# A column operand for the partial sums, maxima negated as they are taken, and a wait of GpSimd on the scaled queries

## The chip, the cores and the metric

The kernel runs on one core of a Trainium2 chip. The metric is the device time of one execution in microseconds (us), as the median of several runs. Engines go by the profile's names: PE is TensorE (PEld its weight loads), DVE is VectorE, ACT is ScalarE, POOL is GpSimd, SP is SyncE.

## What is computed

One inference step of a small hybrid backbone: two layers on 128 context tokens and 512 latent tokens (five tiles of 128 tokens, tile 0 the context), model width 1024. Each layer has a global attention (branch a), a windowed attention with a sink logit per head (branch b) and a gated MLP (branch c), merged by sigmoid gates. The part that matters here is the softmax of the attentions, cut to its core:

```python
qa = apply_rope(rms_norm(br['qa'], lw['q_norm']), cos, sin)
s = jnp.einsum('bqkgd,blkd->bkgql', qblk, k).astype(jnp.float32)
if sink is not None:
    s = jnp.concatenate([s, col], axis=-1)
p = jax.nn.softmax(s, axis=-1)
return jnp.einsum('bkgql,blkd->bqkgd', p.astype(v.dtype), v)
```

## The kernel before

**Products in two halves.** Every large product is made in a 32-bit matmul format whose operands are split in a high and a low half, three matmuls for one (lines 872 to 874, and 924). A unit of weights (128 x 1024) is loaded by SP into one of three raw buffers, rounded by ACT to `w_hi` (line 1130, `split_hi`), and POOL subtracts: `w_lo` = raw - `w_hi` (line 1749, event `split`). The halves lie in a ring of four slots, and PE waits on `w_ready` before it uses a unit.

**The order.** All engines walk one list of events, `ORDER`, and each does its part of an event and waits on semaphores for the rest; so the queue of every engine is fixed when the kernel is built. A wait holds back everything behind it on that engine. `with_splits` places the split events between the others, some events after the ring slot's last use.

**One attention group** (`attention`): ten groups per branch and layer, one for each of two key heads and five query tiles, with four query heads each. For a group of latent queries:
- event `S`: PE makes the scores of a unit in PSUM; units are the cached keys of all four heads (branch a only), then one for each head. DVE takes the maximum (line 1600) and makes its negative, combined with the maximum over the cached keys or the sink (line 1602, one column out, a column as operand). ACT waits for that column and takes the exponential (`ex`, line 1292), with the row sum as a side output; the part over cached keys or the sink has a sum of its own (lines 1284, 1287).
- event `iv`: DVE adds the two partial sums of a head (line 1610) and takes the reciprocal (line 1611); POOL multiplies the probabilities by it (line 1772, tile `p_f_a` or `p_f_b`).
- event `T`: PE waits until all heads of the group are scaled and transposes them (line 1075); ACT copies to `p_hi` (line 1303), DVE makes the rest `p_lo` (line 1616, event `pl`), which also frees the PSUM bank; there are two banks for `T`. `PV` (lines 1086, 1087) is two steps behind `T`. The product's sums go through lines 1310 and 1624 to `o_sum`.

Chunks of gate products (line 924) are mixed in as filler. The last two groups, of the context tile, have one unit `heads` with all four heads: DVE reads the maxima of four heads at once (line 1594), in branch b joins the sinks (line 1596), and negates (line 1597).

```python
after(did(dve.tensor_reduce(best, by_head(ps[:, s, :]), axis=AX.X, op=ALU.max)))
if br == "b":
    after(did(dve.tensor_tensor(best, best, sinks, ALU.max)))
did(dve.tensor_scalar(neg[:, c, :], best, -1.0, None, ALU.mult), neg_made)
```

**The queries.** In `queries_or_keys` DVE rotates the projected queries out of PSUM and writes `q_st`: in branch a it sums squares (line 1435), POOL makes the root (`root`, lines 1732 and 1733), and DVE multiplies (line 1449); in branch b it adds (line 1455). Either raises `staged`. PE then transposes `q_st` (line 1036, event `qt`), and ACT (line 1266) and DVE (line 1578) take the halves. There are ten such writes in a layer, five per branch.

Of the kernel before, what the change touches and what calls it, by code (L numbers as in the profile page):

```python
# [10 lines left out]
ALU = mybir.AluOpType  # L11
ACT = mybir.ActivationFunctionType
AX = mybir.AxisListType
# [10 lines left out]
GRP = 4  # L24
# [535 lines left out]
NO = numbers()  # L560
# [58 lines left out]
def build(nc, a, outs):  # L619
    with ExitStack() as ctx:  # L620
# [44 lines left out]
        neg = sb("neg", [P, 3, GRP])  # L665
        sums = sb("sums", [P, 3, 2, GRP])
# [67 lines left out]
        ps = ctx.enter_context(nc.psum_tensor("ps", [P, BANKS, 512], F32))  # L734
# [18 lines left out]
        sq_ready, v_hi_made, staged = sem("sq_ready"), sem("v_hi_made"), sem("staged")  # L753
        k_hi_made, q_hi_made = sem("k_hi_made"), sem("q_hi_made")
        neg_made, inv_made, over_sum = (sem(n) for n in ("neg_made", "inv_made", "over_sum"))
# [9 lines left out]
        class Tally:  # L765
# [5 lines left out]
            def did(self, instruction, semaphore=None):  # L771
                s = semaphore or self.step
                instruction.then_inc(s, 1)
                self.n[s.name] = self.n.get(s.name, 0) + 1
                return s, self.n[s.name]
# [40 lines left out]
        def by_head(tile):  # L816
            return tile.rearrange("p (h n) -> p h n", h=GRP)
# [10 lines left out]
        with nc.Block() as block:  # L828
# [532 lines left out]
            def _(dve):  # L1361
                tally = Tally(dve_step)
                did = tally.did
# [3 lines left out]
                def after(token):  # L1367
                    dve.wait_ge(*token)
# [93 lines left out]
                for e in ORDER:  # L1462
                    kind = e[0]
# [119 lines left out]
                    elif kind == "S":  # L1583
# [6 lines left out]
                        if unit == "cache":  # L1590
                            did(dve.tensor_reduce(others, by_head(ps[:, s, :]), axis=AX.X, op=ALU.max), neg_made)
                            dve.wait_ge(neg_made, NEG_NO[e])
                        elif unit == "heads":
                            after(did(dve.tensor_reduce(best, by_head(ps[:, s, :]), axis=AX.X, op=ALU.max)))
                            if br == "b":
                                after(did(dve.tensor_tensor(best, best, sinks, ALU.max)))
                            did(dve.tensor_scalar(neg[:, c, :], best, -1.0, None, ALU.mult), neg_made)
                        else:
                            h, n = unit, len(group_slots(br, g)) - (br == "a")
                            after(did(dve.tensor_reduce(best[:, h:h + 1], ps[:, s, 0:n * P], axis=AX.X, op=ALU.max)))  # L1600
                            other = others[:, h:h + 1] if br == "a" else sinks[:, h:h + 1]
                            did(dve.tensor_scalar(neg[:, c, h:h + 1], best[:, h:h + 1], other, -1.0, ALU.max, ALU.mult), neg_made)
                    elif kind == "iv":
# [2 lines left out]
                        heads = slice(0, GRP) if unit == "heads" else slice(unit, unit + 1)  # L1606
                        wait_drained(dve, ("S",) + e[1:])
                        total = sums[:, c, 0, heads]
                        if br == "b" or unit != "heads":
                            after(did(dve.tensor_tensor(total, total, sums[:, c, 1, heads], ALU.add)))  # L1610
                        did(dve.reciprocal(inv[:, c, heads], total), inv_made)  # L1611
                    elif kind == "pl":
# [108 lines left out]
            @block.gpsimd  # L1721
            def _(pool):
                tally = Tally(pool_step)
                did = tally.did
                asked = [0]

                def root(out, src, eps, first=0):
                    asked[0] += 1
                    pool.wait_ge(var_ready, asked[0])
                    n = out.shape[-1]  # L1730
                    mine = with_eps[:, first:first + n]
                    pool.wait_ge(*did(pool.tensor_scalar(mine, src, eps, None, ALU.add)))
                    did(pool.tensor_tensor(out, mine, minus_half[:, 0:n], ALU.pow), rstd_ready)

                def shift(t):
                    pool.wait_ge(rstd_ready, asked[0])
                    pool.wait_ge(*did(pool.tensor_tensor(nmr[:, t:t + 1], mv[:, t, 0:1], rstd[:, t:t + 1], ALU.mult)))
                    did(pool.tensor_scalar(nmr[:, t:t + 1], nmr[:, t:t + 1], -1.0, None, ALU.mult), nmr_ready)

                did(pool.memset(silu_c[:, :, :], 0.0), zeroed)  # L1740
                did(pool.memset(minus_half[:, :], -0.5), zeroed)
                pool.wait_ge(zeroed, 2)
                for e in ORDER:
                    kind = e[0]
                    if kind == "split":
                        n = e[1]
                        r, _ = raw_at(SPLIT_LOAD[n])
                        pool.wait_ge(hi_made, n + 1)
                        did(pool.tensor_tensor(w_lo[:, n % RING, :], raw_tile(r), w_hi[:, n % RING, :], ALU.subtract),  # L1749
                            w_ready)  # L1750
                    elif kind == "ln" and e[1]:
                        _, l, t = e
                        root(rstd[:, t:t + 1], mv[:, t, 1:2], EPS, t)
                        shift(t)
                    elif kind == "ln" and e[1] == 0:
                        for t in ARRIVAL:
                            root(rstd[:, t:t + 1], mv[:, t, 1:2], EPS, t)
                            if t in XN_ON_ACT:
                                shift(t)
                    elif kind in ("ln", "vn"):  # L1760
                        root(rstd[:, :], rstd[:, :], EPS)
                    elif kind == "in" and e[2] in ("q_a", "kv_a"):
                        heads = NKV if e[2] == "kv_a" else HEADS
                        c = NO[("sq", e)] % 2
                        root(rqk[:, c, 0:heads], ssq[:, c, 0:heads], HD * EPS)
                    elif kind == "iv":
                        _, l, br, g, i = e
                        c, unit = GROUP_NO[e[1:4]] % 3, score_units(br, g)[i]
                        heads = slice(0, GRP) if unit == "heads" else slice(unit, unit + 1)
                        part = p_part(br, g)[:, heads, :]  # L1770
                        pool.wait_ge(inv_made, NO[e] + 1)
                        did(pool.tensor_tensor(part, part, inv[:, c, heads].unsqueeze(2).to_broadcast(list(part.shape)), ALU.mult),  # L1772
                            over_sum)
                    elif kind == "og":
                        _, l, br, g = e
                        n = NO[e]
                        wait_drained(pool, ("O",) + e[1:])
                        wait_drained(pool, ("gT", l, br, 2 * GROUPS[g][0] + 1))
                        did(pool.tensor_tensor(og_sum(n), og_sum(n), og_part(g_t, g), ALU.mult), og_ready)
                    elif kind == "ol":  # L1780
                        _, l, br, g = e
                        n = NO[e]
                        pool.wait_ge(o_hi_made, O_MADE[e])
                        did(pool.tensor_tensor(og_part(o_lo, g), og_sum(n), og_part(o_hi, g), ALU.subtract), o_done)
                    elif kind == "y" and e[2] >= 1:
                        _, l, r, j = e
                        wait_drained(pool, e)
                        did(pool.tensor_tensor(merge[:, j, :], merge[:, j, :], gy[:, j % 2, :], ALU.add), merged)  # L1788
                    elif kind == "keep":
                        _, l, n = e  # L1790
                        r, _ = raw_at(KEEP_LOAD[e])
                        pool.wait_ge(keep_hi_made, KEPT[KEEP_LOAD[e]] + 1)
                        did(pool.tensor_tensor(kept_lo[n][:, :], raw_tile(r), kept_hi[n][:, :], ALU.subtract), kept)
                    elif kind == "out" and e[2] == 1 and e[1:] != (DEPTH - 1, 1, T - 1):
                        _, l, _, t = e
                        wait_drained(pool, e)
                        pool.wait_ge(x_alpha, T * l + t + 1)
                        did(pool.tensor_tensor(x[:, t, BW:D], x[:, t, BW:D], scaled[:, t % 2, :], ALU.add), x_summed)
                    elif kind == "st":
                        _, l, t = e  # L1800
                        root(rstd[:, t:t + 1], mv[:, t, 1:2], EPS, t)
                    elif kind == "hl":
                        _, l, t = e
                        pool.wait_ge(hh_ready, KT_D + t + 1)
                        did(pool.tensor_tensor(h_lo[:, :, t * P:(t + 1) * P], hf_of[:, :, :],
                                               h_hi[:, :, t * P:(t + 1) * P], ALU.subtract), h_ready)
# [110 lines left out]
```

## Time and profile before

| | |
|---|---|
| median of 3 runs | 1471.08 us (1470.16 to 1475.82) |
| the profiled execution | 1472.22 us, of which the span is 1470.1 us |
| PE busy | 1392.7 us, 95% of the span |
| POOL busy | 704.0 us, 48% |
| DVE busy | 726.2 us, 49% |
| ACT busy | 638.3 us, 43% |
| the chain that ended last | PE 79%, DVE 4%, POOL 3%, ACT 2%, issue 2% |
| costliest group off PE | line 1749, POOL, 148 splits, 358.1 us |
| granted TensorE clock, mean | 0.987 |

The busy share of an engine is an average over the span; the time of the kernel can only fall where PE stands idle, or runs at a low clock. So the profile is read for PE's idle stretches first: each has a place, a length and a releaser.

### The profile page before, as it was taken

To read this page: it belongs to the slowest core of one execution; us is meant where nothing else is said; L and a number is where in the kernel's file an instruction comes from. 1 tells how busy PE (TensorE), PEld (TensorE's weight loads), DVE (VectorE), ACT (ScalarE), POOL (GpSimd) and SP (SyncE) were. 2 spreads that over 40 slices of the span, in tenths; PEclk is the share of its full clock that TensorE was granted. 3 is DMA by queue.
4 is the path that set the end of the run, shared out by engine and by line. 5 is a ranking of instruction groups with operands and counts; after the bars stand their busy time and mean duration, and the time that the engine had idled before them with its cause. 6 is when DMAs were issued, how large, how long until landed. Compare 5 with 4: busy or idle time off the path is not lost.

```text
span 1470.1 us, 22567 instructions
## 1 busy us (share of the span) xinstructions
PE 1392.7 (95%) x8816; PEld 1276.4 (87%) x8816; DVE 726.2 (49%) x1412; ACT 638.3 (43%) x1298; POOL 704.0 (48%) x520
## 2 busy tenths in 40 slices
PE   5999999999999999999979999999999999999996
PEld 3898989889898898999868988897989989999985
DVE  4687774363663501413774767734546625031057
ACT  4345875335874211224143377752267733121230
POOL 2456665324565334344674556642246453444453
PEclk9999999999999999999989999999999999999999
DMA  8412001122013244343321210011111031225321
GB/s 332 146 47 82 20 30 44 62 72 72 30 44 107 92 147 165 108 186 122 111 98 35 85 58 30 24 63 63 58 59 44 30 129 44 86 72 187 115 87 72
DMA packets 36763, 126.96 MB, mean 86 GB/s; under 512 B 5041, under 2 KB 5681, under 8 KB 36657
## 3 DMA queue, kind: packets, MB, share of 16 engines
q1 hardware_dynamic: 29952, 108.54, 20.9%
q10 hardware_dynamic: 6704, 16.97, 3.2%
q8 instruction: 71, 1.16, 0.3%
q14 instruction: 36, 0.29, 0.1%
HBM read 119.73 MB, written 5.77 MB: 85 GB/s over the span
## 4 chain that ended last, share of the span: by engine, by line
PE 79%; DVE 4%; POOL 3%; ACT 2%; issue 2%; DVEq 0%; POOLq 0%; ACTq 0%
PE ps L924 45%; PE ps L872 6%; PE ps L874 6%; PE ps L873 6%; PE ps L1075 4%; PE ps L1059 3%; PE ps L1061 2%; PE ps L1086 2%; PE ps L1087 2%; POOL w_lo L1749 1%; PE ps L941 1%; ACT p_f_a L1292 1%; PE ps L1094 1%; POOL p_f_a L1772 1%; PE ps L1066 1%
## 5 line engine op out<-in xcount | busy, mean ns | idle before, releaser
L1749 POOL TENSOR_TENSOR w_lo<-raw,w_hi 128x1024 fp32r<-128x1024 f32 x148 | 358.1, 2426 | 361.4 <-ACT w_hi L1130 361.2
L924 PE MATMUL ps<-h_hi,w_hi 128*128 128x320 f32 x1280 | 298.1, 314 | 11.5 <-DVE g_c L1632 3.6
L924 PE MATMUL ps<-h_lo,w_hi 128*128 128x320 f32 x1280 | 293.0, 310 | 0.0
L924 PE MATMUL ps<-h_hi,w_lo 128*128 128x320 f32 x1280 | 292.9, 310 | 0.0
L924 PEld LDWEIGHTS ps<-h_hi,w_hi 128*128 128x128 f32 x1280 | 218.0, 189 | 31.5 <-issue 9.1
L924 PEld LDWEIGHTS ps<-h_hi,w_lo 128*128 128x128 f32 x1280 | 215.7, 189 | 1.7
L924 PEld LDWEIGHTS ps<-h_lo,w_hi 128*128 128x128 f32 x1280 | 215.3, 188 | 1.6
L1130 ACT ACTIVATE w_hi<-raw 128x1024 fp32r<-128x1024 f32 x148 | 153.5, 1054 | 103.8 <-DMA raw<-in_weights 50.5
L1647 DVE TENSOR_TENSOR gy<-ps,sg 128x640 f32<-128x640 f32 x32 | 26.4, 824 | 241.3 <-PE ps L924 241.3
L1600 DVE TENSOR_REDUCE top<-ps 128x1 f32<-128x512 f32 (+1 forms) x128 | 83.9, 655 | 111.3 <-PE ps L1066 78.1
L872 PE MATMUL ps<-w_hi,h_hi 128*128 128x512 f32 (+1 forms) x360 | 130.2, 362 | 4.1 <-POOL w_lo L1749 2.2
L874 PE MATMUL ps<-w_hi,h_lo 128*128 128x512 f32 (+1 forms) x360 | 128.6, 357 | 0.0
L873 PE MATMUL ps<-w_lo,h_hi 128*128 128x512 f32 (+1 forms) x360 | 128.5, 357 | 0.0
L1772 POOL TENSOR_TENSOR p_f_a<-p_f_a,inv 128x640 f32<-128x640 f32 (+1 forms) x68 | 84.3, 1241 | 80.4 <-DVE inv L1611 80.4
L1343 ACT ACTIVATE sg<-ps,pack 128x640 f32<-128x640 f32 x32 | 25.4, 795 | 210.6 <-PE ps L924 210.5
L1772 POOL TENSOR_TENSOR p_f_b<-p_f_b,inv 128x512 f32<-128x512 f32 (+1 forms) x68 | 62.9, 940 | 77.6 <-DVE inv L1611 77.6
L1303 ACT ACTIVATE p_hi<-ps 128x512 fp32r<-128x512 f32 x144 | 85.6, 594 | 31.8 <-PE ps L1075 28.4
L924 PE MATMUL ps<-o_hi,w_hi 128*128 128x320 f32 x384 | 91.4, 320 | 6.9 <-DVE rot_s L1392 6.0
L1788 POOL TENSOR_TENSOR merge<-merge,gy 128x640 f32<-128x640 f32 x32 | 51.2, 1600 | 85.8 <-DVE gy L1647 85.7
L924 PE MATMUL ps<-o_lo,w_hi 128*128 128x320 f32 x384 | 88.7, 312 | 0.0
L924 PE MATMUL ps<-o_hi,w_lo 128*128 128x320 f32 x384 | 88.5, 312 | 0.0
L1059 PE MATMUL ps<-k_hi,q_t 128*128 128x128 f32 (+2 forms) x224 | 81.6, 381 | 7.2 <-ACT p_f_b L1292 4.2
(178 smaller groups left out, 2674.0 us busy)
## 6 DMA issues: line engine op xcount, KB each, us to landing
raw<-in_weights SPq DMA_DIRECT2D x190, 512.0 KB, 3.3
raw_more<-in_weights SPq DMA_DIRECT2D x10, 512.0 KB, 10.6
x<-in_x_sample ACTq DMA_DIRECT2D x6, 512.0 KB, 8.6
x_mid<-x ACTq DMA_DIRECT2D x5, 512.0 KB, 2.6
x<-x_mid ACTq DMA_DIRECT2D x5, 512.0 KB, 6.4
y_sample<-x SPq DMA_DIRECT2D x3, 512.0 KB, 2.9
pack<-in_pack ACTq DMA_DIRECT2D x2, 528.0 KB, 4.6
x<-in_x_sample SPq DMA_DIRECT2D x2, 512.0 KB, 4.9
```

The source lines that it names most:

```text
L872: pe.matmul(out, st_hi, mv_hi, start=start, stop=False)
L873: pe.matmul(out, st_hi, mv_lo, start=False, stop=False)
L874: return pe.matmul(out, st_lo, mv_hi, start=False, stop=stop)
L924: last = pe.matmul(ps[:, s + half, 0:HALF], w[:, u % RING, cols], acts[:, k, half * HALF:(half + 1) * HALF], start=k == 0 and part == 0, s ...
L1059: pe.matmul(ps[:, s, col:col + width], q_t[:, head, t * P:(t + 1) * P], k_hi[:, kv, src], start=True, stop=False)
L1075: last = pe.transpose(ps[:, s, h * P:(h + 1) * P], p_part(br, g)[:, h, i * P:(i + 1) * P], ident)
L1130: did(act.activation(w_hi[:, n % RING, :], raw_tile(r), ACT.Copy), hi_made)
L1303: did(act.activation(p_hi[:, n % 3, :], ps[:, s, :], ACT.Copy), p_hi_made)
L1600: after(did(dve.tensor_reduce(best[:, h:h + 1], ps[:, s, 0:n * P], axis=AX.X, op=ALU.max)))
L1749: did(pool.tensor_tensor(w_lo[:, n % RING, :], raw_tile(r), w_hi[:, n % RING, :], ALU.subtract), w_ready)
L1772: did(pool.tensor_tensor(part, part, inv[:, c, heads].unsqueeze(2).to_broadcast(list(part.shape)), ALU.mult), over_sum)
L1788: did(pool.tensor_tensor(merge[:, j, :], merge[:, j, :], gy[:, j % 2, :], ALU.add), merged)
```

## The change

Three edits, all inside the walks of DVE and POOL:

- In branch a the maxima of the context tile are written negated by the reduction itself, and the second instruction goes. In branch b the reduction stays, and one instruction per head joins the sink (a column operand) and negates, four in place of two.
- The two partial sums of one head are added by `tensor_scalar` with the second sum as a column operand, in place of `tensor_tensor`.
- POOL waits, at each event of projected queries, until DVE has written `q_st`. Everything behind it in POOL's queue waits too, the next split above all.

```diff
@@ -1591,10 +1591,13 @@
                             did(dve.tensor_reduce(others, by_head(ps[:, s, :]), axis=AX.X, op=ALU.max), neg_made)
                             dve.wait_ge(neg_made, NEG_NO[e])
                         elif unit == "heads":
-                            after(did(dve.tensor_reduce(best, by_head(ps[:, s, :]), axis=AX.X, op=ALU.max)))
-                            if br == "b":
-                                after(did(dve.tensor_tensor(best, best, sinks, ALU.max)))
-                            did(dve.tensor_scalar(neg[:, c, :], best, -1.0, None, ALU.mult), neg_made)
+                            if br == "a":
+                                did(dve.tensor_reduce(neg[:, c, :], by_head(ps[:, s, :]), axis=AX.X, op=ALU.max, negate=True), neg_made)
+                            else:
+                                after(did(dve.tensor_reduce(best, by_head(ps[:, s, :]), axis=AX.X, op=ALU.max)))
+                                for h in range(GRP):
+                                    last = dve.tensor_scalar(neg[:, c, h:h + 1], best[:, h:h + 1], sinks[:, h:h + 1], -1.0, ALU.max, ALU.mult)
+                                did(last, neg_made)
                         else:
                             h, n = unit, len(group_slots(br, g)) - (br == "a")
                             after(did(dve.tensor_reduce(best[:, h:h + 1], ps[:, s, 0:n * P], axis=AX.X, op=ALU.max)))
@@ -1606,7 +1609,9 @@
                         heads = slice(0, GRP) if unit == "heads" else slice(unit, unit + 1)
                         wait_drained(dve, ("S",) + e[1:])
                         total = sums[:, c, 0, heads]
-                        if br == "b" or unit != "heads":
+                        if unit != "heads":
+                            after(did(dve.tensor_scalar(total, total, sums[:, c, 1, heads], None, ALU.add)))
+                        elif br == "b":
                             after(did(dve.tensor_tensor(total, total, sums[:, c, 1, heads], ALU.add)))
                         did(dve.reciprocal(inv[:, c, heads], total), inv_made)
                     elif kind == "pl":
@@ -1759,10 +1764,14 @@
                                 shift(t)
                     elif kind in ("ln", "vn"):
                         root(rstd[:, :], rstd[:, :], EPS)
+                    elif kind == "in" and e[2] == "q_b":
+                        pool.wait_ge(staged, NO[e] + 1)
                     elif kind == "in" and e[2] in ("q_a", "kv_a"):
                         heads = NKV if e[2] == "kv_a" else HEADS
                         c = NO[("sq", e)] % 2
                         root(rqk[:, c, 0:heads], ssq[:, c, 0:heads], HD * EPS)
+                        if e[2] == "q_a":
+                            pool.wait_ge(staged, NO[e] + 1)
                     elif kind == "iv":
                         _, l, br, g, i = e
                         c, unit = GROUP_NO[e[1:4]] % 3, score_units(br, g)[i]
```

DVE's queue in the attention of branch a, layer 0, where the third head's sum of a group is added and the next group's cached keys come in; before (`sums` are the row sums, `inv` their reciprocals, `drained` a PSUM bank given back):

```order
L1616 TENSOR_TENSOR p_lo_last<-ps,p_hi 128x512 [waits p_hi_made]
L1610 TENSOR_TENSOR sums<-sums 128x1 [waits drained1]
L1611 RECIPROCAL inv<-sums 128x1 [waits dve_step]
L1624 TENSOR_TENSOR o_sum<-ps,o_sum 64x256 [waits o_low_made,filled4]
L1624 TENSOR_TENSOR o_sum<-ps,o_sum 64x256 [waits o_low_made]
L1591 TENSOR_REDUCE top<-ps 128x4 [waits filled1]
L1616 TENSOR_TENSOR p_lo_a<-ps,p_hi 128x512 [waits p_hi_made,neg_made]
L1610 TENSOR_TENSOR sums<-sums 128x1 [waits drained0]
L1611 RECIPROCAL inv<-sums 128x1 [waits dve_step]
```

In the changed kernel the same rows stand there in the same order and with the same waits, but those of L1610 read `TENSOR_SCALAR sums<-sums 128x1` (L1613 there); nothing moved.

DVE's queue at the context tile of branch a, layer 0, before:

```order
L1611 RECIPROCAL inv<-sums 128x1 [waits dve_step]
L1594 TENSOR_REDUCE top<-ps 128x4 [waits filled0]
L1597 TENSOR_SCALAR neg<-top 128x4 [waits dve_step]
L1594 TENSOR_REDUCE top<-ps 128x4 [waits filled1]
L1597 TENSOR_SCALAR neg<-top 128x4 [waits dve_step]
L1616 TENSOR_TENSOR p_lo_a<-ps,p_hi 128x512 [waits p_hi_made]
L1616 TENSOR_TENSOR p_lo_last<-ps,p_hi 128x512 [waits p_hi_made]
```

and now:

```order
L1616 RECIPROCAL inv<-sums 128x1 [waits dve_step]
L1595 TENSOR_REDUCE neg<-ps 128x4 [waits filled0]
L1595 TENSOR_REDUCE neg<-ps 128x4 [waits filled1]
L1621 TENSOR_TENSOR p_lo_a<-ps,p_hi 128x512 [waits p_hi_made]
L1621 TENSOR_TENSOR p_lo_last<-ps,p_hi 128x512 [waits p_hi_made]
```

Two instructions are gone, and the first `p_lo` stands right behind the reductions.

POOL's queue at the queries of branch a, layer 0, now (before, the rows are the same without `staged`):

```order
L1737 TENSOR_SCALAR with_eps<-ssq 128x8 [waits var_ready,staged]
L1738 TENSOR_TENSOR rqk<-with_eps,minus_half 128x8 [waits pool_step]
L1754 TENSOR_TENSOR w_lo<-raw,w_hi 128x1024 [waits hi_made,staged]
L1737 TENSOR_SCALAR with_eps<-ssq 128x8 [waits var_ready]
L1738 TENSOR_TENSOR rqk<-with_eps,minus_half 128x8 [waits pool_step]
L1754 TENSOR_TENSOR w_lo<-raw,w_hi 128x1024 [waits hi_made,staged]
```

Of the 20 added waits, 16 fall on a split (3 and 5 in branch a of layers 0 and 1, 4 and 4 in branch b), two on a root, and two are followed at once by another wait. PE's, ACT's and SP's queues are the same in both kernels.

## Rows read from the trace of the kernel before

**Rows 1.** Whom PE waited for, whole run: us in total, times, longest us.
```profile
PE ps L1075 <- POOL p_f_a L1772: 5.4, 4, 2.4
...
PE ps L1036 <- DVE q_st L1449: 1.3, 1, 1.3
...
PE ps L1075 <- DVE p_lo_last L1616: 0.5, 2, 0.2
```

**Rows 2.** Timeline around 181 to 188 us, all engines: start, us, engine, line, operation [idle before].
```profile
181.20 2.38 POOL L1749 TENSOR_TENSOR w_lo<-raw,w_hi 128x1024 fp32r<-128x1024 f32 x1
...
181.35 2.25 DVE L1610 TENSOR_TENSOR sums<-sums 128x1 f32<-128x1 f32 x1
...
182.73 0.59 ACT L1303 ACTIVATE p_hi<-ps 128x512 fp32r<-128x512 f32 x1
...
184.94 0.46 PE L924 MATMUL ps<-h_hi,w_lo 128*128 128x320 f32 x2
...
185.34 0.69 DVE L1616 TENSOR_TENSOR p_lo_a<-ps,p_hi 128x512 fp32r<-128x512 f32 x1
...
186.37 1.25 POOL L1772 TENSOR_TENSOR p_f_a<-p_f_a,inv 128x640 f32<-128x640 f32 x1 [1.24 <-DVE inv L1611]
...
187.77 0.63 PE L1075 MATMUL ps<-ident_r,p_f_a 128*128 128x128 f32 x4 [2.37 <-POOL p_f_a L1772]
```

**Rows 3.** Lines 1610 and 1602, all instances: ns min/median/max, first and last start, forms.
```profile
L1610 DVE TENSOR_TENSOR sums<-sums x132: 130/150/2256, 132.1 to 1175.5; 128x1 f32<-128x1 f32 x128, 128x4 f32<-128x4 f32 x4
...
L1602 DVE TENSOR_SCALAR neg<-top x64: 212/214/215, 129.3 to 945.0; 128x1 f32<-128x1 f32 x64
L1602 DVE TENSOR_SCALAR neg<-top,pack x64: 212/214/217, 348.0 to 1162.9; 128x1 f32<-128x1 f32 x64
```

**Rows 4.** Timeline, 134 to 135.5 us, POOL and DVE.
```profile
134.13 1.25 POOL L1772 TENSOR_TENSOR p_f_a<-p_f_a,inv 128x640 f32<-128x640 f32 x1 [0.38 <-DVE inv L1611]
...
134.91 0.21 DVE L1602 TENSOR_SCALAR neg<-top 128x1 f32<-128x1 f32 x1
135.06 0.34 DVE L1610 TENSOR_TENSOR sums<-sums 128x1 f32<-128x1 f32 x1
```

**Rows 5.** Timeline, 221 to 230 us: the context tile of branch a, layer 0.
```profile
223.72 2.39 POOL L1749 TENSOR_TENSOR w_lo<-raw,w_hi 128x1024 fp32r<-128x1024 f32 x1
223.72 2.41 DVE L1597 TENSOR_SCALAR neg<-top 128x4 f32<-128x4 f32 x1
...
226.05 0.68 DVE L1616 TENSOR_TENSOR p_lo_a<-ps,p_hi 128x512 fp32r<-128x512 f32 x1
...
226.78 0.66 PE L1075 MATMUL ps<-ident_r,p_f_a 128*128 128x128 f32 x4 [1.50 <-DVE p_lo_a L1616]
```

**Rows 6.** Three stretches: us, busy us of PE, PEld, DVE, ACT, POOL; PEclk, DMA, GB/s.
```profile
187.77:226.78 39.01, 37.51 (x247) 34.68 (x247) 30.29 (x73) 30.53 (x87) 24.46 (x21) 1.00 0.04 15
913.65:954.26 40.61, 39.11 (x246) 35.99 (x247) 30.28 (x73) 30.65 (x87) 24.48 (x21) 0.96 0.04 14
849.30:856.10 6.80, 6.80 (x27) 6.55 (x27) 2.68 (x5) 2.77 (x4) 4.68 (x2) 0.51 0.30 91
```

**Rows 7.** Timeline, 843.5 to 852 us: the last queries of branch a, layer 1.
```profile
844.09 2.79 DVE L1449 TENSOR_TENSOR q_st<-rot_c,rqk 128x512 f32<-128x512 f32 x1 [1.46 <-POOL rqk L1733]
...
847.03 0.63 PE L1036 MATMUL ps<-ident_r,q_st 128*128 128x128 f32 x4 [1.27 <-DVE q_st L1449]
847.25 1.41 DVE L1578 SCALAR_TENSOR_TENSOR q_t<-ps,q_t 64x512 fp32r<-64x512 f32 x2 [0.37 <-ACT q_t L1266]
...
848.76 0.53 PE L924 MATMUL ps<-h_hi,w_hi 128*128 128x320 f32 x2 [1.11 <-issue]
```

**Rows 8.** Line 1449, all instances: ns min/median/max, first and last start, form.
```profile
L1449 DVE TENSOR_TENSOR q_st<-rot_c,rqk x10: 693/2809/2827, 72.5 to 844.1; 128x512 f32<-128x512 f32 x10
```

**Rows 9.** Timeline: a split of branch a's queries and PE's first use.
```profile
90.10 2.40 POOL L1749 TENSOR_TENSOR w_lo<-raw,w_hi 128x1024 fp32r<-128x1024 f32 x1
...
99.42 0.54 PE L924 MATMUL ps<-h_hi,w_hi 128*128 128x320 f32 x2
```

**Rows 10.** Timeline, 311 to 319 us: the queries of branch b, layer 0.
```profile
315.11 2.40 POOL L1749 TENSOR_TENSOR w_lo<-raw,w_hi 128x1024 fp32r<-128x1024 f32 x1 [10.91 <-ACT w_hi L1130]
...
317.01 1.05 DVE L1455 TENSOR_TENSOR q_st<-rot_c,rot_s 128x512 f32<-128x512 f32 x1
```

## The prediction, made before the changed kernel was run

> **What bounds the kernel now.** I read the table of the profile first: PE is busy for 1392.7 us of 1470.1, so only PE's idle stretches, and stretches at a low clock, can give time back. The view of who waited for whom, for PE alone, lists the idle by releaser. Of its 23 lines, four speak of work that the change touches: the transposes of line 1075 wait 5.4 us in 4 places for POOL's scaling of the probabilities and 0.5 us in 2 for a late `p_lo` [rows 1], 1.50 us (and as much again in layer 1) for the first `p_lo` of the context tile [rows 5], and the transposes of the queries 1.3 us in one place [rows 1]. Then I read the timeline around each. The two layers run alike, so a stall of layer 0 comes back some 726 us later.
>
> *The stall at 187.77.* POOL starts a split at 181.20 that ends at 183.58. DVE starts the sum of two columns at 181.35 and ends at 183.60: 2.25 us for one element per partition [rows 2], where the median of that line is 0.150 us [rows 3]. The reader should see that the two ends fall together: DVE was held until POOL had finished. All that DVE does next is late, `p_lo` at 185.34, then the group's last sum, then POOL's scaling at 186.37, and PE, free at about 185.4, starts the transposes at 187.77 after 2.37 us idle [rows 2].
>
> *The stall at 226.78.* The same with another instruction: the negation of four columns starts with a split at 223.72 and takes 2.41 us, `p_lo` starts at 226.05, and PE has stood for 1.50 us [rows 5].
>
> **The change, part by part.**
>
> *The sums by column operand (128 of them).* Is the new form held by POOL too? The trace has the same form, one column in, a column operand, one column out, in line 1602: 128 instances, none over 0.217 us [rows 3], while POOL is busy for 48% of the span. One pair shows it within half a microsecond: POOL scales from 134.13 to 135.38; the column form starts at 134.91 and takes 0.21 as ever, the old sum starts at 135.06 and takes 0.34, that is to 135.40 [rows 4]. So I take 0.214 us for each. Against 0.150 it costs 0.064 more in a free place, 8.2 us of DVE time over 128, beside PE's work: DVE is idle for half of the span.
>
> The Trainium skill ("SBUF — State Buffer", section "Who interferes with whom") says that a `tensor_scalar` can enter a mode that takes both ports and is then shut out by a GpSimd instruction until its end, as a `tensor_tensor` with two inputs in SBUF is. Read plainly, that would hold the new form as well, and leave the stall at 187.77 where it is. The four-column negation agrees with it, the one-column form here does not; it is the first rival below.
>
> What is the stall worth then? Before, a product's rest at 185.34 leads to the scaling at 186.37, 1.03 us later, and that to PE at 187.77, 1.40 later [rows 2]. Now DVE is free 2 us sooner, and `p_lo` can start when ACT's copy ends, 182.73 + 0.59 = 183.32. POOL is still in its split until 183.58, then scales the head before, 1.25 us [rows 4], to 184.83; the last head's scaling, ready at 183.35 + 1.03 = 184.38, starts at about 184.8. PE starts at 184.8 + 1.40 = 186.2. So 1.6 of the 2.37 us go, and 0.8 stay, since POOL's own split is next in line. In both layers: **-3.2 us**. Bounds: 2.0 in all if POOL is 0.6 later than that, 4.7 if nothing stays.
>
> *The clock behind it.* In layer 0 the stretch from the end of this stall to the next takes 39.01 us at clock 1.00; in layer 1 the same work takes 40.61 us at 0.96, with part of it at the lower of the two levels (1.2 for 2.4 GHz), right behind the 2.38 us of idle time [rows 6]. With 0.8 us idle I expect no fall there: **-1.6 us**. The same idle time fell to either side in one execution, so this is worth between 0 and 3.2 in another.
>
> *The negated maxima, branch a.* Two negations go in each layer. The second reduction then ends about 223.0, and `p_lo` can start there instead of at 226.05. PE needs the bank at 226.78 - 1.50 = 225.28, so that stall goes whole [rows 5], and so does the 0.2 us at the next transposes [rows 1], as ACT's exponentials, which waited for the negation, start 3 us sooner. 2 x (1.50 + 0.23) = **-3.5 us**. Bounds: 2 x 1.0 and 2 x 1.73. What is late next there: nothing that the rows show before PE has work.
>
> *The context tile of branch b.* Four column forms in place of two instructions: an extra 0.2 to 0.3 us of DVE, four times in the run. PE shows no wait there now. 0, at most +0.4.
>
> *POOL's wait on the queries.* Branch a's multiplication takes 0.693 us when free and 2.809 in the median of ten [rows 8]; it starts 0.14 behind a split and is held. Now it goes first. It gives DVE some 2.1 us back, eight times. Does PE wait for it? Once: at 847.03, 1.27 us [rows 7]. But the next gate chunk at 848.76 waits for a bank that DVE gives back when it has taken the fourth queries, and that runs from 847.25 to 848.66, released by ACT, not by the multiplication [rows 7]. PE reaches the transposes 1.5 us sooner, and waits 1.5 us longer at the chunk. I take 0; the bounds are 0 and -1.3.
>
> What it costs: each split that carries the wait starts when the multiplication ends: +0.9 us in branch a, 8 times. In branch b, 2 x (1.1 + 1.2 + 2.7): the largest is at 315.11, where two waits of queries stand before one split, and the later query is written at 317.01 + 0.69 = 317.7 [rows 10, 8]. That is 17.2 us of delay on POOL in all. What is queued behind: the next root (its squares come 3 us later), the raw buffer that SP refills, and PE. The nearest use by PE in these stretches is that of a split which ends at 92.50 and is first needed at 99.42 [rows 9]: 6.9 us of room against 0.9. **0**, at most +0.5.
>
> *The small losses.* The first group's sums and the sum before the gate product of branch b stand right before something that PE waits for: 4 x 0.05 = **+0.2 us**.
>
> Sum: -3.2 - 1.6 - 3.5 + 0.2 = -8.1 us against the profiled execution's 1472.22: **1464.2 us** (rounded up from 1464.1). That execution stands 1.14 above the median shown, 1471.08; without the clock's share the median would come to 1464.6, so the two agree. It is 0.47% below the median. A measurement of this kernel tells about 0.5% from no change, and 0.5% lies at 1463.7: the forecast sits just inside.
>
> **The rivals.**
>
> *The column form is held as well.* Only the context tile gains: 1472.2 - 3.5 = 1468.7. For it: the four-column form of the same operation was held 2.41 us [rows 5]. Against it: 128 of 128 in rows 3.
>
> *More of the clock comes back.* From 849.30 to 856.10 PE works without a gap at 0.51 of its clock [rows 6], behind the two idle pieces at 847.03 and 848.76. If the new order of these waits leaves the clock up, half of 6.8 us goes: 1464.2 - 3.4 = 1460.8. For it: the same stall fell on either side in layers 0 and 1. Against it: the idle time there stays as long as it was, 2.4 us or more in one piece.
>
> *Half of the gain.* POOL, with scalings and a split in its queue, is the late one at both stalls, and only about half of them goes; the clock falls as before: 1472.2 - 4 = 1468.2.
>
> *The splits come late: slower.* If the waits hold POOL past PE's first use of the units, their delay reaches PE. If all of it did, 17.2 us: 1464.2 + 17.2 = 1481.4. It decides when a split's room falls below its delay; the least room is 6.9 against 0.9, and where the delay is 2.7 the unit is used later still. So it would need DVE to be some 6 us later with the queries than it is.
>
> **How the numbers follow.** Forecast (both holds go, the clock as above): 0.56, of which I put a quarter below 1463.7, since the clock's term can be 0 to 3.2 and the residue of the stall is worked out to a few tenths only. More of the clock: 0.28. The column form held: 0.05. Half of the gain: 0.07. Splits late: 0.04. Faster by over 0.5%: 0.14 + 0.28, rounded to 0.43. Slower: 0.04. Same: the rest, 0.53. The range reaches from the clock's rival to the form that is held, 1460.6 to 1468.4; what lies outside is the slow case and half of the two weak ones.
>
> **What would show it.** In the changed kernel's trace: the sums all at 0.21 us, with none over 0.25; the reductions of branch a's context tile writing `neg`, and no 2.4 us behind them; PE's wait for POOL's scaling down from 5.4 to some 2.3 us, its waits for the first `p_lo` of the context tile gone; PE's busy time the same but for the clock; line 1449 at 0.69 us in all ten; PE's gap before the chunk at 848.76 grown as the one at 847.03 goes; splits behind the queries later by 0.9 us with no wait of PE on `w_lo` near them. I am wrong if a sum still takes 2 us, if PE waits for `w_lo` in the query stretches, or if a new stall follows the two that go.

## The result, and the profile after

The changed kernel takes 1460.9 us (median of 5 runs, 1459.78 to 1461.67), the kernel before 1471.08 us on the same chip (5 runs, 1470.16 to 1475.82). The ratio is 0.9927, with a 95% interval of 0.9913 to 0.9940: faster by 0.73%, more than the 0.5% that a measurement tells apart. The forecast was 1464.2 us, in a range of 1460.6 to 1468.4; it gave 0.53 to a change too small to tell and 0.43 to one of over 0.5%. The time lies in the range, at its lower end, and the gain is of the size that was held the less likely.

The profiled execution took 1461.58 us, with a span of 1459.8: 10.3 us less than before, at a mean clock of 0.989 for 0.987. PE is busy for 1388.0 us (1392.7 before), DVE for 688.2 (726.2), POOL for 703.5 (704.0).

The lines that the change touches, all instances in the kernel after (ns min/median/max, first and last start, forms), one answer for each line:

```profile
L1613 DVE TENSOR_SCALAR sums<-sums x128: 194/203/215, 131.5 to 1156.5; 128x1 f32<-128x1 f32 x128
```
```profile
L1595 DVE TENSOR_REDUCE neg<-ps x4: 672/676/681, 219.8 to 941.7; 128x4 f32<-128x512 f32 x4
```
```profile
L1449 DVE TENSOR_TENSOR q_st<-rot_c,rqk x10: 691/692/693, 71.9 to 841.2; 128x512 f32<-128x512 f32 x10
```

They answer to [rows 3, 5, 8]. No sum takes over 0.215 us (2.256 before), no negation of four columns is left in branch a, and all ten multiplications of line 1449 take 0.69 us (2.81 in the median before).

Whom PE waited for, kernel after (us in total, times, longest), against [rows 1]:

```profile
PE ps L924 <- DVE rot_s L1392: 6.0, 2, 3.0
...
PE ps L1059 <- ACT p_f_a L1292: 2.8, 2, 1.4
...
PE ps L924 <- issue: 2.6, 1, 2.6
...
PE ps L1075 <- POOL p_f_a L1781: 2.4, 4, 0.8
```

The transposes wait 2.4 us for POOL's scaling, in one stall of 0.8 and one of 0.4 per layer; before it was 5.4. The waits for a late `p_lo` and for `q_st` are no longer there. `rot_s` is untouched at 6.0. The wait of scores for ACT's `p_f_a` grew from 1.9 us to 2.8.

*The stall at 187.77* [rows 2] is now at 185.81. Timeline of the kernel after, around it:

```profile
180.85 2.38 POOL L1754 TENSOR_TENSOR w_lo<-raw,w_hi 128x1024 fp32r<-128x1024 f32 x1
```
```profile
180.95 0.20 DVE L1613 TENSOR_SCALAR sums<-sums 128x1 f32<-128x1 f32 x1
```
```profile
183.20 2.46 POOL L1781 TENSOR_TENSOR p_f_a<-p_f_a,inv 128x640 f32<-128x640 f32 x2
```
```profile
185.81 0.63 PE L1075 MATMUL ps<-ident_r,p_f_a 128*128 128x128 f32 x4 [0.81 <-POOL p_f_a L1781]
```

The same sum that was held for 2.25 us starts 0.10 us into the split and takes 0.20. POOL is now the late one: its split ends at 183.23 and two scalings follow without a gap.

*The context tile* [rows 5]: the transposes that stood at 226.78 start at 223.17 with no idle time. Two stretches of the kernel after (us; busy us of PE, PEld, DVE, ACT, POOL; clock; DMA; GB/s), the same work as in the first two rows of [rows 6]:

```profile
185.81:223.17 37.36, 37.36 (x247) 34.77 (x247) 27.62 (x71) 30.81 (x91) 23.44 (x21) 1.00 0.06 17
907.17:944.53 37.36, 37.36 (x247) 34.73 (x248) 27.62 (x71) 30.79 (x91) 23.43 (x21) 1.00 0.06 17
```

Layer 0 gives 39.01 - 37.36 = 1.65 us, layer 1, which had a low clock there, 40.61 - 37.36 = 3.25.

**Where the 10.3 us came from.** Starts of the same instruction of PE in the two profiles, us:

| instruction (its releaser) | before | after | gained here |
|---|---|---|---|
| first transposes behind the heads' start (POOL scaling) | 138.80 | 138.33 | 0.47 |
| the stall on POOL's scaling, layer 0 | 187.77 | 185.81 | 1.49 |
| transposes of the keys behind the context tile, layer 0 | 273.94 | 269.84 | 2.14 |
| first product of line 966 after its 5.2 us wait, layer 1 | 755.43 | 751.47 | -0.14 |
| gate chunk that waits for ACT's `g_t`, layer 1 | 814.95 | 812.10 | -1.11 |
| gate chunk behind the last queries | 848.76 | 845.92 | -0.01 |
| next scores that wait for ACT's `p_f_a` | 857.93 | 852.89 | 2.20 |
| the stall on POOL's scaling, layer 1 | 913.65 | 907.17 | 1.44 |
| line 924 behind the wait for `rot_s`, layer 1 | 1029.78 | 1019.56 | 3.74 |
| last instruction | 1470.1 | 1459.8 | 0.08 |

Of the 3.74 us, 2.14 are the context tile's, as in layer 0, and 1.60 the clock behind the stall that shrank. Two rows had no term in the prediction: 2.20 gained between 848.76 and 857.93 (third row of [rows 6]), and 1.11 lost ahead of 814.95. Both go with the clock: 0.86 before and 1.00 after from 840 to 865 us, 0.83 and 0.77 from 745 to 775 (table further down). Of what a higher clock gave back behind 848.76, 0.93 us went into the wait for `p_f_a`, which was 0.46 before and is 1.39. The 0.47 us lie ahead of nearly all that the change touches, and are within chance: the transposes at 187.77 stand at 186.74 and 189.81 us in two further profiles of the unchanged kernel.

### The profile page after: what moved, and what is told of

The parts are those of the page before. It is cut to its first block and busy times, and to the rows that moved or that the text cites. A ratio compares the mean times of both kernels' runs of the same rounds, so it can differ in the third digit from the quotient of the medians.

```text
span 1459.8 us, 22589 instructions
## 1 busy us (share of the span) xinstructions
PE 1388.0 (95%) x8816; PEld 1272.9 (87%) x8816; DVE 688.2 (47%) x1416; ACT 638.1 (44%) x1298; POOL 703.5 (48%) x520
```

## The experiments

The theory after the result: **T**, the two holds were worth about what was forecast, and the rest is clock that comes back behind the last queries of layer 1. Rivals: **W**, POOL's waits bring more than the 0 forecast, by PE's 1.27 us and by the clock behind it; **N**, the negated maxima bring more than 3.5. The first four kernels ran on one chip (before: 1470.75 us, 23 runs), the next three on another (before: 1470.77 us, 9 runs), the last four on a third, one run each.

**Sums alone, in the kernel before.**

```diff
-                        if br == "b" or unit != "heads":
+                        if unit != "heads":
+                            after(did(dve.tensor_scalar(total, total, sums[:, c, 1, heads], None, ALU.add)))
+                        elif br == "b":
                             after(did(dve.tensor_tensor(total, total, sums[:, c, 1, heads], ALU.add)))
```

> The kernel before with the sums by column operand alone. Theory of stalls: the wait of PE at 187.8 us falls from 2.37 to 0.8 in each layer and nothing else moves, -3.0 us; with the low stretch of the clock behind it in layer 1 gone, -4.6, so 1466.5 to 1468.1 us. No sum takes over 0.22 us. Rival, the parts help each other (a late POOL or DVE at one stall feeds the next): less than 2 us, 1469.5 or more. Rival, DVE's extra 0.05 us for each of 128 sums reaches PE: no gain at all, 1471 or more.

Measured: 1464.42 us (1462.56 to 1465.52), ratio 0.9954 (0.9939 to 0.9969): 6.3 us less. The timeline of PE in this kernel shows one hold gone and the other left, as it should:

```profile
184.06 0.63 PE L1075 MATMUL ps<-ident_r,p_f_a 128*128 128x128 f32 x4 [0.81 <-POOL p_f_a L1774]
```
```profile
223.12 0.66 PE L1075 MATMUL ps<-ident_r,p_f_a 128*128 128x128 f32 x4 [1.56 <-DVE p_lo_a L1618]
```

From 840 to 865 us the clock stays at 1.00, though PE waits there for the queries as before (1.27 and 1.11 us). So it was not POOL's waits that kept it up, and the sums are worth 6.3 us (4.6 to 9.0 by the interval of the ratio) where the two terms of the sum came to 4.8.

There is one more place. Behind the wait for `rot_s` in layer 0 this kernel has no low stretch, and the changed kernel has one. PE's timeline at that wait and at the next, in this kernel's second profile:

```profile
300.46 0.56 PE L924 MATMUL ps<-o_hi,w_hi 128*128 128x320 f32 x2 [2.99 <-DVE rot_s L1392]
...
305.16 0.56 PE L924 MATMUL ps<-o_hi,w_hi 128*128 128x320 f32 x2 [0.48 <-DVE merge L1642]
```

The work between the two starts takes 4.70 us (4.71 in the first profile of this kernel). In the changed kernel it takes 6.24 (298.21 to 304.45), as in the kernel before (302.30 to 308.54): 1.5 us that this kernel gains there and the changed one does not. Why is not shown.

**Negated maxima alone, branch a, in the kernel before.**

```diff
-    after(did(dve.tensor_reduce(best, by_head(ps[:, s, :]), axis=AX.X, op=ALU.max)))
+    if br == "a":
+        did(dve.tensor_reduce(neg[:, c, :], by_head(ps[:, s, :]), axis=AX.X, op=ALU.max, negate=True), neg_made)
...
```

> The kernel before with the maxima of branch a's context tile negated by the reduction alone. The prediction's own size: -3.5 us, 1467.6. Theory that a stall costs more than its idle time as the row gives it (the row counts from the modelled end of the last matmul, some 0.16 us after the next one could have started): the changed kernel shows 2.14 per layer between the same landmarks, so -4.3, 1466.8, and the same 2.1 per layer here. Rival, part of the 2.14 comes from the other edits: 1.7 per layer here.

Measured: 1467.63 us (1465.39 to 1471.06, 11 runs), ratio 0.9978 (0.9967 to 0.9989): 3.1 us less, between 1.6 and 4.9. The stalls at the context tile are gone from the trace and the one on POOL's scaling stands at 2.37. At its place the edit gives what the theory said: in layer 1 it is 85.63 us from the stall on POOL's scaling to the transposes of the keys (914.89 to 1000.52) where it was 87.76 (913.65 to 1001.41), both with one fall of the clock: 2.1 us, not 1.7. So N is right at the place, by 0.4 us a layer. The whole run shows less, and its interval holds 3.5 as well as 4.3. Part of the rest shows in the one profile: behind the wait for `rot_s` in layer 0 the work that took 6.24 us takes 7.48. With the 6.3 us of the sums the two parts make 9.4, where the changed kernel without the waits stands 9.0 below the kernel before on the same chip.

**POOL's waits alone, in the kernel before.**

```diff
+                    elif kind == "in" and e[2] == "q_b":
+                        pool.wait_ge(staged, NO[e] + 1)
...
                         root(rqk[:, c, 0:heads], ssq[:, c, 0:heads], HD * EPS)
+                        if e[2] == "q_a":
+                            pool.wait_ge(staged, NO[e] + 1)
```

> The kernel before with POOL's waits on the queries alone. Theory of the prediction: nothing, 1471.1, the idle time at 847 us goes in one place and comes back whole at the next; PE's idle time the same. Rival, the two idle pieces made one leave the clock up from 849 to 856 us: 2 to 3.4 us faster, 1467.7 to 1469, with no low stretch there in the profile. Rival, delayed splits reach PE: slower, with a wait of PE on w_lo near 90, 315, 830 or 1043 us.

Measured: 1469.8 us (1468.09 to 1475.25, 12 runs), ratio 0.9991 (0.9982 to 1.0001). All ten multiplications are at 0.69 us, and PE does not wait for them. What is gained there is lost in the next wait (PE's timeline):

```profile
852.39 0.53 PE L924 MATMUL ps<-h_hi,w_hi 128*128 128x320 f32 x2 [2.58 <-issue]
```

One stall of 2.58 in place of 1.27 and 1.11 (with 0.6 us of work between them): nothing gained that stands clear of noise, as forecast. The clock from 840 to 865 us is 0.86, as before, and PE's waits on `w_lo` are those of the kernel before, 2.6 and 2.2 us in total, so both rivals fall.

**The changed kernel without the waits.** The diff is the one above, taken out of it.

> The changed kernel without POOL's waits. If the waits carry nothing: 1460.9 as the changed kernel. If they are what keeps the clock up behind the last queries of layer 1: 2 to 3.4 us slower, 1463 to 1464.3, with a low stretch near 846 to 853 us. If the low stretches only fall by the chance of each execution, this and the run before it scatter, and the mean clock of single executions, not the edit, tells the slow from the fast.

Measured: 1461.76 us (1459.97 to 1462.76), ratio 0.9934 (0.9919 to 0.9949). The changed kernel run again on the next chip gave 0.9936 (0.9922 to 0.9949, below). W falls from both sides: the waits carry nothing, and cost nothing that these runs can tell.

Against the sums alone on the same chip (1464.42 us) this kernel adds the negated maxima and branch b's columns: 2.7 us less, where the place gives 4.3. Most of the difference is the clock behind `rot_s` in layer 0, where the 4.7 us of the sums alone are 6.23 again (298.04 to 304.27 here).

**Branch a's negation column by column, with an immediate, in the kernel before.** Is it one element per partition, or the column operand, that keeps the new form free?

```diff
-    did(dve.tensor_scalar(neg[:, c, :], best, -1.0, None, ALU.mult), neg_made)
...
+        for h in range(GRP):
+            last = dve.tensor_scalar(neg[:, c, h:h + 1], best[:, h:h + 1], -1.0, None, ALU.mult)
+        did(last, neg_made)
```

> The kernel before, but the context tile's negation of branch a is four instructions of one column each, with an immediate and no column operand, in place of one of four columns. It asks what frees an instruction from POOL's hold. Theory, one element per partition is never held, whatever the operands: the sixteen instructions take 0.2 us each, also that which starts with the split at 223.7 us (2.41 us before), and PE's wait of 1.5 us at 226.8 is gone. Rival, the column operand is what frees it: one of them in each layer takes about 2.4 us, and the wait stays.

Measured: 1467.11 us in one run, 3.7 below the median before. The line, all instances, and what POOL and DVE did at the first four (timeline):

```profile
L1600 DVE TENSOR_SCALAR neg<-top x16: 143/144/154, 220.1 to 947.9; 128x1 f32<-128x1 f32 x16
```
```profile
219.52 1.25 POOL L1776 TENSOR_TENSOR p_f_a<-p_f_a,inv 128x640 f32<-128x640 f32 x1 [1.36 <-DVE inv L1615]
```
```profile
220.06 0.34 DVE L1600 TENSOR_SCALAR neg<-top 128x1 f32<-128x1 f32 x4
```

All four start and end inside POOL's scaling, which ends at 220.77: not held, without any column operand. None of the sixteen came to stand inside a split, as the expectation had it. But the kernel before has the four-column form at the same place, inside the same scaling, and there it was held (timeline, kernel before):

```profile
221.82 1.25 POOL L1772 TENSOR_TENSOR p_f_a<-p_f_a,inv 128x640 f32<-128x640 f32 x1 [1.36 <-DVE inv L1611]
...
222.36 0.73 DVE L1597 TENSOR_SCALAR neg<-top 128x4 f32<-128x4 f32 x1
```

The scaling ends at 223.07 and the negation at 223.09; in a free place the same four columns take 0.17 us (441.85). So for this operation one element per partition against four decides, and not the column operand; two and three were not tried.

**Queries one place earlier, in the changed kernel.** A large wait that another order might mend is left: the one for `rot_s`, 2.99 us in each layer.

```diff
-    out.extend([qs[1], *whole(("y", l, 0, 2)), ("kt", l, "b", 4), ("kt", l, "b", CACHE), qs[2], *whole(("y", l, 0, 3)),
+    out.extend([qs[1], qs[2], *whole(("y", l, 0, 2)), ("kt", l, "b", 4), ("kt", l, "b", CACHE), *whole(("y", l, 0, 3)),
```

> The changed kernel with the event of the second queries of branch b moved ahead of the projection chunk in front of which it stood, in both layers. It goes for the wait of 2.99 us on line 1392 that the change left in each layer. DVE then reads these queries while PE is in that chunk: the wait goes, some 0.7 us may come back at the next chunk, whose bank is freed by the chunk before. If only the idle time counts: -4.5 us, 1456.4; if the low stretch of the clock behind each wait goes as well, -7.5, 1453.4. Rival, the next chunks then wait for DVE's merge each, and nothing is gained: 1460 or more.

Measured: 1454.96 us (1451.27 to 1455.13, 4 runs), ratio 0.9893 (0.9878 to 0.9908). It beats both kernels, the changed one by 5.5 us. PE's timeline where the wait stood, in the first layer:

```profile
292.81 0.56 PE L924 MATMUL ps<-o_hi,w_hi 128*128 128x320 f32 x2 [0.48 <-DVE merge L1645]
```

The time lies between the two that were expected, 1456.4 and 1453.4. The 2.99 us became 0.48 in each layer (layer 1 at 1010.68), twice 2.5 us gone, and from 290 to 315 and 1015 to 1040 us the clock is 1.00 for 0.93 in the changed kernel.

**The changed kernel again.**

> The changed kernel once more, beside its variant on the same chip: 1460.9. It also gives more executions in which to see where the low stretches of the clock fall. If the fall behind the last queries of layer 1 is chance, one of these executions may show it.

Measured: 1460.46 us (1459.64 to 1464.63), ratio 0.9936 (0.9922 to 0.9949). Its profiled execution, the 1464.63, has a short low stretch there: the clock from 840 to 865 us is 0.93.

**Both kernels and the sums alone once more, for their profiles.** What stayed open was the clock. Two profiles of the kernel before (the first expectation says that five profiles with the old sums had the low stretch; there were four), one with the sums, one of the changed kernel:

> The kernel before once more, for its profile alone: where does the clock fall? Theory S (the held sums set the clock behind the last queries of layer 1): in all five profiles with the old sums that stretch, near 849 us, was low, so it is low again, some 6.8 us at 0.51. Theory C (chance): it was low in two of five with the new sums, so it may be absent. Both: behind the 2.4 us stall on POOL's scaling a low stretch in one or both layers.

> The same kernel once more. Theory S: the stretch near 849 us is low again, which makes it seven of seven with the old sums. Theory C: it is absent here or in the run ahead. Both: time within 1467 to 1476 us.

> Before with the sums by column operand alone, once more. Theory S: no low stretch near 845 us, as in its first profile. Theory C: there in about half of the profiles. Both: none behind the two stalls of 0.8 us on POOL's scaling. Time 1462 to 1466 us.

> The changed kernel once more (it was absent in one of its profiles near 849 us and there in the other). Theory S: absent or of one unit (some 3 us). Theory C: as long as in the kernel before (6.8 us) in some. Both: none behind the stalls of 0.8 us, one behind the 3.0 us stall near 1019 us. Time 1459 to 1462 us.

Measured, in one run each: 1475.81, 1470.04, 1464.51 and 1464.83 us; the last lies outside the 1459 to 1462 that were expected. Three stretches of the second of the two profiles of before (columns as above):

```profile
745.00:775.00 30.00, 20.41 (x105) 17.34 (x104) 20.54 (x32) 12.12 (x20) 23.66 (x21) 0.79 0.30 105
840.00:865.00 25.00, 20.84 (x136) 18.95 (x135) 15.86 (x32) 15.50 (x35) 14.19 (x10) 1.00 0.26 84
900.00:925.00 25.00, 22.63 (x138) 20.73 (x138) 18.54 (x44) 18.33 (x48) 15.15 (x13) 0.93 0.07 22
```

The granted clock in the same stretches of all profiles whose order of work is the changed kernel's or the one before (a profile's own shift of a few us moves the second decimal):

| profile | 180:200 | 900:925 | 745:775 | 840:865 |
|---|---|---|---|---|
| before | 1.00 | 0.93 | 0.83 | 0.86 |
| negated maxima alone | 0.91 | 0.93 | 0.84 | 0.86 |
| waits alone | 0.91 | 0.93 | 0.88 | 0.86 |
| one column each | 1.00 | 0.93 | 0.83 | 0.86 |
| before, second | 0.91 | 0.93 | 0.88 | 0.86 |
| before, third | 1.00 | 0.93 | 0.79 | 1.00 |
| changed | 1.00 | 1.00 | 0.77 | 1.00 |
| changed, second | 1.00 | 1.00 | 0.83 | 0.93 |
| changed, third | 1.00 | 1.00 | 0.77 | 1.00 |
| changed, no waits | 1.00 | 1.00 | 0.77 | 1.00 |
| sums alone | 1.00 | 1.00 | 0.77 | 1.00 |
| sums alone, second | 1.00 | 1.00 | 0.77 | 1.00 |

Two things can be read from it.

1. The first two columns: behind the stall of 2.37 us on POOL's scaling the clock fell in 9 of 12 places; behind the same stall at 0.8 us in none of 12. In layer 1 it fell each time, in layer 0 in half.
2. The last two columns go together. Where the stretch near 849 stays at full clock, the one ahead of it, near 767, is low for longer. Five of six profiles with the old sums have the first pattern (a low stretch near 849), five of six with the new sums the second; but one profile of the unchanged kernel has the second too. So theory S, as a rule without exception, is refuted; C, as even chance, is the less likely, though six profiles a side are few. The second pattern is cheaper by 2.20 - 1.11 = 1.09 us, by the table of starts above.

When PE arrives does not tell the two apart. It starts the chunk behind the last queries at 845.85 us in the profile of one column each, which has the low stretch, and at 845.86 in that of the changed kernel without waits, which has none; in the kernel before at 848.76 with it and at 848.77 (third profile) without.

So T holds for the stall on POOL's scaling, and not for the rest: the maxima were worth more at their place than forecast, and the clock differs between the two kernels at the stall itself, behind the last queries and near 767 us.

## Why the prediction was right, and where it was wrong

*The form by column is not held: right.* 128 of 128 at 0.215 us or less. The Trainium skill ("VectorE: DVE Perf Modes", section "Mode 2×_2P — use both read ports for one tensor") gives as a condition for a `tensor_scalar` to take both ports "outermost non-unit dim even (or odd and equal for src and dst)". The trace agrees for four columns, which have an even one and were held for 2.41 us. One element per partition has no dimension above one, a case that the section does not name; the runs show it free, with a column operand (0.20 us inside a split) or with an immediate (0.34 us for four of them inside a scaling). The first rival left this condition out.

*The stall on POOL's scaling, -3.2: right in kind, 0.2 to 0.3 too much.* 1.49 and 1.44 us went, 0.81 and 0.83 us stay, where 0.8 was worked out.

*The clock behind it, -1.6: the first term that failed.* For this pair of profiles the term came out exact, 1.60 us, in layer 1 alone. But the sum took one profile's case for the kernel's: the fall came in 9 of 12 places, so the kernel before pays for it 2 x 0.75 x 1.6 = 2.4 us on average, and the changed one nothing. The prediction had the bound (0 to 3.2), and put its own value in the middle, with a row that showed one fall in two.

*The point it was counted from.* The prediction took its 8.1 us off the profiled execution, 1.14 us over the median, and gave as the reason that the median would lack the clock's share. But the fall in layer 1 came in all six profiles with the old sums, in those of 1467.11 and 1470.04 us too, so the median has it as well. From the median the same terms give 1463.0 us, a gain of 0.55%.

*The clock behind the last queries, 0: the second.* "The idle time there stays as long as it was" is right (2.57 us in one piece after), and yet 2.2 us came back, against 1.1 lost near 767. The rival "more of the clock" gave 1460.8 us and 0.28; its time was right, and its reason was wrong: the waits on POOL do nothing to it (the kernel without them has the same clock). What goes with it in most profiles are the new sums; by the shares above (one of six profiles in the cheaper pattern with the old sums, five of six with the new) this is worth some 1.09 x 4/6 = 0.7 us, an estimate. How the sums would do it is not shown, and an earlier arrival alone is not it, as the four starts above show.

*The negated maxima, -3.5: the third.* Both stalls went as described, but 2.14 us came back in each layer, not 1.73, so 4.3 in all. The price had been read from the idle figure alone. The windows show the rest. Of the 1.65 us up to the first transposes 1.50 were idle, and of the 0.49 behind them (226.78:273.94 took 47.16 us, 223.17:269.84 takes 46.67) 0.23. So the stalls cost more than their idle figures, here by 0.15 and 0.26 us. A likely reason, not tested, is that PE's ends are modelled, and that the first instructions behind a stall take longer: 0.66 us for the transposes at 226.78, 0.60 after. The upper bound given, 2 x 1.73, excluded the truth at the place. In the whole run less of it shows, 3.1 us in the kernel before and 2.7 on top of the sums, since the clock takes a part back elsewhere.

*Context tile of branch b and the small losses: right.* No stall is new there; the first transposes wait 0.37 us for POOL where it was 0.32 to 0.33, which is the 0.05 of a sum.

*POOL's waits, 0 and 0: right*, by both experiments. The split at 315.11 [rows 10] now starts at 313.74, which is 313.74 - (315.11 - 4.10) = 2.7 us later, as forecast, and PE does not wait for it. "Splits late" falls with that.

The sum with the measured terms: 2.9 for the stall, 2.4 and 0.7 of clock, 4.3 for the context tile, less 0.2: 10.1 us, against 10.2 between the medians. The prediction's 8.1 (6.9 from the median) lacked 0.8 of clock at the stall, 0.7 behind the queries and 0.8 at the context tile, less 0.3. That the sum comes within 0.1 us is in part luck: its two terms of clock are shares out of six profiles, and what the clock took back behind `rot_s` in single kernels is not in it. The forecast lay 0.5 us above the 1463.7 from which a gain can be told; the three errors of 0.7 to 0.8 us all lay on the same side, and the point it was counted from added 1.1.

## What to carry to other kernels

Price a stall from the window around it, same work with and without, and not from its idle figure. Price the clock behind a stall from several profiles of the same kernel, since one execution shows one outcome per place, and count the share of profiles in which it fell, in each layer by itself. Count a change from the median, unless several profiles show that the profiled execution has something the others lack. On DVE, an operation on one element per partition ran free beside POOL as a `tensor_scalar` (128 of 128 at 0.215 us or less), and was held for nearly a whole split as a `tensor_tensor` of two columns (2.25 us), as was a `tensor_scalar` over four columns (2.41).

## What the runs showed of the hardware that was not expected

- The operand that is a column of SBUF does not count as a second input here: 128 such sums took 0.194 to 0.215 us with POOL busy 48% of the span, where the two-column form took up to 2.256 [rows 3].
- A low stretch of PE's clock cost 1.6 us behind the stall on POOL's scaling, and came behind 2.37 us of idle time in 9 of 12 places. With the same work and the same idle times at the place (1.27 and 1.11 us, to 0.01), the unchanged kernel showed 0.86 from 840 to 865 us in one profile and 1.00 in another.
- Low stretches trade places: a longer one near 767 us comes with none near 849, in eleven of twelve profiles one or the other, with the second of the changed kernel in between. So a gain or a loss at one stretch of one profile can't be put down to what stands at that place without a look at the others.
- An idle time of 2.99 us does not always bring one: behind the wait for `rot_s` the work up to the next wait took 5.98 to 7.48 us in 22 of 24 places (two layers of the twelve profiles above), and 4.70 and 4.71 in layer 0 of the two profiles of the sums alone.
